# Attention value products in two passes instead of three, and a rewritten mixer order, in an fp32-accurate encoder layer

## The reference, cut to what matters

```python
h = _rms(x, g_mix[l]); z = h @ w_in[l]          # q | k | v | f | gate a | gate b
y_a = _window_attention(q, k, v, sink[l], rel_bias) @ w_branch_a[l]
y_b = _fourier_mix(f) @ w_branch_b[l]
x = x + (gate_a * y_a + gate_b * y_b) @ w_out[l]
```

## Time and profile before

| | us |
|---|---|
| median of three runs | 1013.02 |
| the profiled execution, whole | 1014.11 |
| its span from first to last instruction | 1012.3 |
| PE busy in the span | 997.7 (99%) |
| PEld busy | 885.7 (87%) |
| DVE busy | 679.0 (67%) |
| ACT busy | 440.1 (43%) |
| granted PE clock, mean | 0.995 of 2.4 GHz |

### The profile page before, as it was taken

The page is one execution under the profiler, slowest core; times in us unless marked ns, Lnnn a source line. Parts: engine busy times, 40 slices in busy tenths (PEclk is TensorE's granted clock), DMA queues, the critical chain, the costliest instruction groups (busy, mean ns, idle before and its releaser), DMA issues. The chain is left out here.

```text
span 1012.3 us, 16276 instructions
## 1 busy us (share of the span) xinstructions
PE 997.7 (99%) x5872; PEld 885.7 (87%) x5872; DVE 679.0 (67%) x924; ACT 440.1 (43%) x656; POOL 198.1 (20%) x113
## 2 busy tenths in 40 slices
PE   8999999999999999999999999999999999999997
PEld 7789999999788888888888888888999999978887
DVE  5778999999534346667765555458899999943332
ACT  5344444446322325346664334334445454633322
POOL 2452333340011110000000001324234333001101
PEclk9999999999999999999999999999999999999999
DMA  6423334323433364212213343322333332333222
GB/s 210 132 66 94 116 92 120 87 83 96 124 96 90 115 171 125 63 42 62 63 42 89 98 124 104 104 84 72 96 108 100 110 97 83 89 117 96 88 68 84
DMA packets 191816, 98.81 MB, mean 98 GB/s; under 512 B 13384, under 2 KB 190616, under 8 KB 191648
## 3 DMA queue, kind: packets, MB, share of 16 engines
q1 hardware_dynamic: 190560, 95.50, 32.3%
q10 hardware_dynamic: 1216, 2.78, 0.8%
HBM read 96.15 MB, written 2.11 MB: 97 GB/s over the span
## 5 line engine op out<-in xcount | busy, mean ns | idle before, releaser
L575 ACT ACTIVATE w_hi<-raw 128x1024 fp32r<-128x1024 f32 (+2 forms) x202 | 181.5, 902 | 231.6 <-PE bank L1496 155.2
L953 DVE TENSOR_TENSOR w_lo<-raw,w_hi 128x1024 fp32r<-128x1024 f32 (+2 forms) x138 | 150.0, 1089 | 145.7 <-ACT w_hi L575 144.2
L1595 PE MATMUL bank<-t_lo,w_hi 128*128 128x256 f32 x896 | 224.7, 283 | 0.0
L1593 PE MATMUL bank<-t_hi,w_hi 128*128 128x256 f32 x896 | 224.6, 283 | 0.0
L1595 PEld LDWEIGHTS bank<-t_lo,w_hi 128*128 128x128 f32 x896 | 172.0, 192 | 0.2
L1593 PEld LDWEIGHTS bank<-t_hi,w_hi 128*128 128x128 f32 x896 | 172.0, 192 | 0.2
L1430 POOL TENSOR_TENSOR ssum<-ssum,sq 128x512 f32<-128x512 f32 x27 | 41.4, 1533 | 535.2 <-ACT sq L612 534.4
L1599 PE MATMUL bank<-t_hi,w_lo 128*128 128x256 f32 x896 | 144.0, 283 | 0.0
L1484 PE MATMUL bank<-a_hi,w_hi 128*128 128x512 f32 (+1 forms) x374 | 140.6, 380 | 1.7 <-ACT a_hi L575 1.7
L1485 PE MATMUL bank<-a_lo,w_hi 128*128 128x512 f32 (+1 forms) x374 | 139.4, 377 | 0.0
L1599 PEld LDWEIGHTS bank<-t_hi,w_lo 128*128 128x128 f32 x896 | 123.6, 192 | 0.0
(11 more groups left out here) (230 smaller groups left out, 1494.6 us busy)
## 6 DMA issues: line engine op xcount, KB each, us to landing
raw<-in_w_down_dram SPq DMA_DIRECT2D x48, 384.0 KB, 3.0
raw_b<-in_w_up_dram SPq DMA_DIRECT2D x64, 256.0 KB, 3.7
raw<-in_w_up_dram SPq DMA_DIRECT2D x64, 256.0 KB, 3.6
raw<-in_w_up_dram SPq DMA_DIRECT2D x24, 512.0 KB, 3.9
raw<-in_w_in_dram SPq DMA_DIRECT2D x22, 512.0 KB, 3.7
raw<-in_w_down_dram SPq DMA_DIRECT2D x32, 128.0 KB, 2.2
raw<-in_w_out_dram SPq DMA_DIRECT2D x8, 512.0 KB, 3.4
x_rows<-in_x_dram SPq DMA_DIRECT2D x4, 512.0 KB, 7.8
```

The lines of the kernel that those rows point to most:

```text
L575: return nc.scalar.activation(dst, src, ACT.Copy, scale=scale)
L953: vec.tensor_tensor(w_lo[:, s, 0:nk, :], raw[:, s, 0:nk, :], w_hi[:, s, 0:nk, :].bitcast(F32), ALU.subtract).then_inc(w_lo_ready, 1)
L1593: nc.tensor.matmul(out_ap, w_hi[:, slot, at_ + k, :], hi[:, k, :], start=first and k == 0, stop=False, skip_group_check=not first)
L1595: nc.tensor.matmul(out_ap, w_hi[:, slot, at_ + k, :], lo_[:, k, :], start=False, stop=False, skip_group_check=not first)
```

## The change

v is kept in one tile `v_st` with a stationary block for each group: for group 0 columns 0 to 63 are v_hi and 64 to 127 are v_lo, for group 1 the other way round. `values` then takes two products, v_st x pt_hi and v_st x pt_lo, and leaves the part of v_hi in one half of the partitions of bank 3 and the part of v_lo in the other. (The lo x lo part comes with it.) The halves are added by two new operations at the last `values` of a unit: ACT copies the v_lo half of the bank to the other half of the partitions of `y_t` (`o_shifted`), DVE adds the bank's v_hi half to it (`o_added`). A new step `keep u`, one or more steps later in the list, has ACT copy the sum to `qo_hi` and DVE write `qo_lo`. The next unit's first `values` waits for `o_added` instead of `o_lo_ready`. The split of v is two operations on each engine instead of one. The list is rewritten, `B_B` starts with bank 0, and three waits follow it.

```diff
-B_B = [1, 0, 7]
+B_B = [0, 1, 7]
 MIXER:
-    positions 2; channels 3; q 2; turn_v; positions 3; q 3;
-    scores 0 0; scores 0 1; gate_b 0 0 0; gate_b 0 0 1; scores 0 2; scores 0 3; max 0; gate_b 0 0 2; exp 0;
+    positions 2; channels 3; q 2; turn_v; positions 3; scores 0 0; scores 0 1; q 3;
+    gate_b 0 0 0; scores 0 2; scores 0 3; max 0; gate_b 0 0 1; gate_b 0 0 2; exp 0;
     scores 1 0; normalize 0; gate_b 0 0 3; gate_b 0 1 0; scores 1 1; turn 0 0; turn 0 1; scores 1 2;
-    gate_b 0 1 1; values 0 0; scores 1 3; max 1; values 0 1; exp 1; normalize 1; gate_b 0 1 2; gate_b 0 1 3;
-    branch_b 0 0 0; sigmoid 0;
-    scores 2 0; scores 2 1; turn 1 0; branch_b 0 0 1; turn 1 1; branch_b 0 1 0; values 1 0; values 1 1;
-    scores 2 2; scores 2 3; max 2; take_b 0 0; exp 2; normalize 2; branch_b 0 1 1; gate_b 1 0 0; gate_b 1 0 1;
+    gate_b 0 1 1; values 0 0; scores 1 3; max 1; gate_b 0 1 2; values 0 1; exp 1; normalize 1; gate_b 0 1 3;
+    keep 0; branch_b 0 0 0; sigmoid 0;
+    scores 2 0; scores 2 1; turn 1 0; branch_b 0 0 1; turn 1 1; branch_b 0 1 0; values 1 0; scores 2 2; scores 2 3;
+    values 1 1; max 2; take_b 0 0; exp 2; normalize 2; keep 1; branch_b 0 1 1; gate_b 1 0 0; gate_b 1 0 1;
     take_b 0 1; gate_b 1 0 2; gate_b 1 0 3; turn 2 0; turn 2 1;
-    scores 3 0; scores 3 1; gate_b 1 1 0; values 2 0; turn 2 2; values 2 1; scores 3 2; scores 3 3; max 3;
-    exp 3; normalize 3; gate_b 1 1 1; gate_b 1 1 2; gate_b 1 1 3; values 2 2; sigmoid 1;
+    scores 3 0; scores 3 1; gate_b 1 1 0; values 2 0; turn 2 2; scores 3 2; scores 3 3; values 2 1; max 3;
+    exp 3; normalize 3; gate_b 1 1 1; gate_b 1 1 2; values 2 2; gate_b 1 1 3; keep 2; sigmoid 1;
     scores 4 0; branch_b 1 0 0; turn 3 0; turn 3 1; scores 4 1; branch_b 1 0 1; values 3 0; turn 3 2;
-    values 3 1; scores 4 2; scores 4 3; max 4; exp 4; take_b 1 0; branch_b 1 1 0; normalize 4; values 3 2;
-    branch_b 1 1 1; gate_b 2 0 0;
-    scores 5 0; scores 5 1; take_b 1 1; gate_b 2 0 1; turn 4 0; turn 4 1; gate_b 2 0 2; gate_b 2 0 3;
-    values 4 0; values 4 1; turn 4 2; scores 5 2; scores 5 3; max 5; exp 5; normalize 5; gate_b 2 1 0;
-    values 4 2; gate_b 2 1 1; gate_b 2 1 2; gate_b 2 1 3; branch_b 2 0 0; turn 5 0; turn 5 1;
-    scores 6 0; scores 6 1; values 5 0; turn 5 2; values 5 1; scores 6 2; scores 6 3; max 6; exp 6;
-    branch_b 2 0 1; values 5 2; normalize 6; branch_b 2 1 0; branch_b 2 1 1; sigmoid 2; take_b 2 0; take_b 2 1;
+    scores 4 2; scores 4 3; values 3 1; max 4; exp 4; take_b 1 0; branch_b 1 1 0; normalize 4; values 3 2;
+    branch_b 1 1 1; keep 3; gate_b 2 0 0;
+    scores 5 0; scores 5 1; take_b 1 1; gate_b 2 0 1; turn 4 0; turn 4 1; gate_b 2 0 2; values 4 0; gate_b 2 0 3;
+    turn 4 2; values 4 1; scores 5 2; scores 5 3; max 5; exp 5; normalize 5; gate_b 2 1 0;
+    values 4 2; gate_b 2 1 1; keep 4; gate_b 2 1 2; gate_b 2 1 3; branch_b 2 0 0; turn 5 0; turn 5 1;
+    scores 6 0; scores 6 1; branch_b 2 0 1; values 5 0; turn 5 2; scores 6 2; scores 6 3; values 5 1; max 6; exp 6;
+    branch_b 2 1 0; values 5 2; normalize 6; branch_b 2 1 1; keep 5; sigmoid 2; take_b 2 0; take_b 2 1;
     gate_b 3 0 0; gate_b 3 0 1; turn 6 0;
     scores 7 0; turn 6 1; gate_b 3 0 2; scores 7 1; values 6 0; scores 7 2; scores 7 3; values 6 1; max 7;
-    exp 7; normalize 7; gate_b 3 0 3; gate_b 3 1 0; ...
+    exp 7; normalize 7; gate_b 3 0 3; keep 6; gate_b 3 1 0; ...
-    ... values 7 1; branch_b 3 1 1; sigmoid 3; take_b 3 0; take_b 3 1;
+    ... values 7 1; branch_b 3 1 1; keep 7; sigmoid 3; take_b 3 0; take_b 3 1;

 ACT, last values of a unit:
-    copy(qo_hi[rows_v, :, block nb], banks[B_O][rows_v, :]).then_inc(o_hi_ready, 1)
+    if u == 0: act.wait_ge(y_lo_ready, N_FGROUPS)
+    if u >= N_KV: act.wait_ge(o_lo_ready, u - N_KV + 1)
+    copy(y_t[half_rows(kv), :], banks[B_O][half_rows(1 - kv), :]).then_inc(o_shifted, 1)
+ACT, keep u:
+    act.wait_ge(o_added, u + 1)
+    copy(qo_hi[half_rows(kv), :, block nb], y_t[half_rows(kv), :]).then_inc(o_hi_ready, 1)
 DVE, last values of a unit:
-    dve.wait_ge(o_hi_ready, u + 1); lo(qo_lo[...], banks[B_O][rows_v, :], qo_hi[...]).then_inc(o_lo_ready, 1)
+    dve.wait_ge(o_shifted, u + 1)
+    vec.tensor_tensor(y_t[half_rows(kv), :], banks[B_O][half_rows(kv), :], y_t[half_rows(kv), :], ALU.add).then_inc(o_added, 1)
+DVE, keep u:
+    dve.wait_ge(o_hi_ready, u + 1)
+    lo(qo_lo[...], y_t[half_rows(kv), :], qo_hi[...]).then_inc(o_lo_ready, 1)
 PE, values:
-    if b == 0 and u >= 1: pe.wait_ge(o_lo_ready, u)
+    if b == 0 and u >= 1: pe.wait_ge(o_added, u)
     pe.wait_ge(pt_hi_ready, t + 1)
-    nc.tensor.matmul(o_bank, v_hi[:, blk, :], pt_hi[:, t % 2, :], ...)
-    nc.tensor.matmul(o_bank, v_lo[:, blk, :], pt_hi[:, t % 2, :], ...)
+    nc.tensor.matmul(o_bank, v_st[:, kv, blk, :], pt_hi[:, t % 2, :], ...)
     pe.wait_ge(pt_lo_ready, t + 1)
-    nc.tensor.matmul(o_bank, v_hi[:, blk, :], pt_lo[:, t % 2, :], ...).then_inc(pt_used, 1)
+    nc.tensor.matmul(o_bank, v_st[:, kv, blk, :], pt_lo[:, t % 2, :], ...).then_inc(pt_used, 1)
 PE, gate_b, first quarter of granule n:
-    pe.wait_ge(out_read, O_B + n - 2 if n else O_B)
+    pe.wait_ge(out_read, O_B + n - 2 if n > 1 else O_B - 1 + n)
 PE, loop behind the mixer list:
-    pe.wait_ge(out_read, o - 3 + SLOTS * pair)
+    pe.wait_ge(out_read, o - (2 if j == 2 else 3) + SLOTS * pair)
```

More of the change, by code:

```diff
@@ L185 @@
-    turn 7 1; branch_b 3 0 0; branch_b 3 0 1; values 7 0; branch_b 3 1 0; values 7 1; branch_b 3 1 1;
+    exp 7; normalize 7; gate_b 3 0 3; keep 6; gate_b 3 1 0; gate_b 3 1 1; gate_b 3 1 2; gate_b 3 1 3; turn 7 0;
+    turn 7 1; branch_b 3 0 0; branch_b 3 0 1; values 7 0; branch_b 3 1 0; values 7 1; branch_b 3 1 1; keep 7;
     sigmoid 3; take_b 3 0; take_b 3 1;
@@ L325, in build @@
         kp_lo, _ = reuse("kp_lo", [P, N_KV, SEQ], F32R)
-        v_hi, _ = reuse("v_hi", [P, TB, P], F32R)
-        v_lo, _ = reuse("v_lo", [P, TB, P], F32R)
+        v_st, _ = reuse("v_st", [P, N_KV, TB, P], F32R)
         bias, bias_at = reuse("bias", [P, N_HEADS, 3 * BLK], F32)
@@ L372, in build @@
         proj_hi_ready, tab_hi_ready, exp_ready = sem("proj_hi_ready"), sem("tab_hi_ready"), sem("exp_ready")
+        o_shifted, o_added = sem("o_shifted"), sem("o_added")
         pt_hi_ready, o_hi_ready, ab_hi_ready = sem("pt_hi_ready"), sem("o_hi_ready"), sem("ab_hi_ready")
@@ L851, in _ @@
                         act.wait_ge(v_turned, 1)
-                        copy(v_hi[:, :, :], banks[B_CH][:, :]).then_inc(v_hi_ready, 1)
+                        v_rows = banks[B_CH][:, :].rearrange("p (t d) -> p t d", t=TB)
+                        for v in range(N_KV):
+                            last = copy(v_st[:, v, :, half_rows(v)], v_rows[:, :, half_rows(v)])
+                        last.then_inc(v_hi_ready, 1)
                     elif kind == "channels":
@@ L884, in _ @@
                         if b == len(window(nb)[0]) - 1:
-                            rows_v = slice(kv * HD, (kv + 1) * HD)
                             act.wait_ge(pt_used, turn_index(u, b) + 1)
-                            copy(qo_hi[rows_v, :, nb * BLK:(nb + 1) * BLK],
-                                 banks[B_O][rows_v, :].rearrange("p (c q) -> p c q", c=GQ)
-                                 ).then_inc(o_hi_ready, 1)
+                            if u == 0:
+                                act.wait_ge(y_lo_ready, N_FGROUPS)
+                            if u >= N_KV:
+                                act.wait_ge(o_lo_ready, u - N_KV + 1)
+                            copy(y_t[half_rows(kv), :], banks[B_O][half_rows(1 - kv), :]).then_inc(o_shifted, 1)
+                    elif kind == "keep":
+                        u = step[1]
+                        nb, kv = u // N_KV, u % N_KV
+                        act.wait_ge(o_added, u + 1)
+                        copy(qo_hi[half_rows(kv), :, nb * BLK:(nb + 1) * BLK],
+                             y_t[half_rows(kv), :].rearrange("p (c q) -> p c q", c=GQ)).then_inc(o_hi_ready, 1)
                     elif kind == "gate_b" and step[3] == 3:
@@ L1278, in _ @@
                         dve.wait_ge(v_hi_ready, 1)
-                        lo(v_lo[:, :, :], banks[B_CH][:, :].rearrange("p (t d) -> p t d", t=TB),
-                           v_hi[:, :, :]).then_inc(v_lo_ready, 1)
+                        v_rows = banks[B_CH][:, :].rearrange("p (t d) -> p t d", t=TB)
+                        for v in range(N_KV):
+                            last = lo(v_st[:, v, :, half_rows(1 - v)], v_rows[:, :, half_rows(v)],
+                                      v_st[:, v, :, half_rows(v)])
+                        last.then_inc(v_lo_ready, 1)
                     elif kind == "channels":
@@ L1343, in _ @@
                         if b == len(window(nb)[0]) - 1:
-                            rows_v, cols = slice(kv * HD, (kv + 1) * HD), slice(nb * BLK, (nb + 1) * BLK)
-                            dve.wait_ge(o_hi_ready, u + 1)
-                            lo(qo_lo[rows_v, :, cols],
```

(21 more changed lines are left out.)

1 line of the change is left out of this document (removed).

## The result

The changed kernel is slower. Its median is 1020.46 us over six runs (1018.73 to 1022.84), against 1013.2 for the kernel before over six runs in the same measurement. The ratio is 1.0078, with a 95% interval of 1.0065 to 1.0090. So the change costs 7.3 us by the medians and 7.9 (6.6 to 9.1) by the ratio. A second measurement of the same kernel gave 1.0081 (1.0068 to 1.0095).

What follows compares the result with a forecast made beforehand. PE was taken to set the time, busy 158.5 of 160 us in the mixer. Net waits of 10.35 us less 4.5 for twenty removed products gave +5.8, a median of 1018.8 us, range 1011.8 to 1022.3.

Steps and rivals of the forecast that it cites:

- Items 1 and 2: Start: scores 0 0 wait 1.1 for v_lo, scores 0 3 wait 2.0 for q 3's rest; net +1.6 us.
- Item 3: Unit 1: chain of 6.3 against PE's 5.2 until turn 1 0, +1.0; later pt_lo 0.25 more.
- Item 4: Unit 2: values 2 0 wait about 0.65 for pt_lo (0.3 before), scores 3 2 wait 0.4; +0.75 us.
- Item 5: Values 3 0, keep 2 before sigmoid 1: wait 1.2, and 0.45 for pt_lo; +1.55 us.
- Item 6: Values 4 0 with one gate step above it instead of two: DVE 4.35 against PE 3.0, +1.35 us.
- Item 7: Unit 4's last block: gate_b 2 0 3 moved later, 3.7 against PE's 3.2, and exp 5 later too; +0.65 us.
- Item 8: Values 5 0, keep 4 before gate_b 2 1 3 on ACT: wait 1.7, 0.35 behind it for scores; net +1.3 us.
- Item 9: Units 5 and 6: 0.8 up to turn 6 0; keep 5 delays pt_lo and scores 7 1's reading by 1.1; +1.9 us.
- Rival (a): Later holes do not open, PE gains 4.5 and pays only 1.6 at the start: 1010.1 us, faster; chance 0.14.
- Rival (b): About half of the later holes open: 1013 us, no change; chance 0.10.
- Rival (d): The removed products' time is not saved: 4.5 more, 1023 us; chance 0.14 together with the clock rival.
- Rival (c): Clock falls once or twice behind the waits, 1.2 to 1.7 each: 1020.0 to 1022.2; 0.14 with the products-not-saved rival.

Runs made afterwards that it cites:

- s1: Kernel before with three products and the old list, only the start and the banks new: ratio 1.0024, stretch 111.4 without its clock fall.
- p1: Kernel before without the product v_lo x pt_hi and nothing in its place, old list: ratio 0.9979, mixer stretch 107.9 us.
- n2: Kernel before with the new list, banks and waits, without v_lo x pt_hi and nothing in its place: ratio 1.0038, stretch 112.0 without its clock fall.
- e1: Changed kernel with the old list, banks and waits, keeps placed late: ratio 0.9984 to the kernel before, mixer stretch 108.4 us.
- e3: Changed kernel with only the keeps moved later, behind max u+2: ratio 1.0044 to the kernel before, stretch 112.5 without its clock fall.
- e2: Kernel before, three products, with the new list (without keep), new banks and waits: ratio 1.0069, stretch 113.8 without its clock fall.
- e4: Changed kernel with only the start put back (q 3 first again): ratio 1.0055 to the kernel before, stretch 113.6 without its clock fall.
- c3: Two products, late keeps, old list with covering gate and branch steps moved earlier from the start, new banks: ratio 1.0028 to the kernel before, stretch 114.1.
- c2: Two products, late keeps, old list and banks, covering steps moved earlier only from values 3 0 on: ratio 0.9989 to the kernel before, stretch 108.7.
- b1: Two products, late keeps, old list, with sigmoids later and exp 5 behind values 4 2: ratio 0.9987 to the kernel before, stretch 108.85.
- b2: Two products, late keeps, old list, with exp 5 behind values 4 2 and values 1 1 one step later: ratio 0.9978, 1010.6 us.

## Why the prediction was right, and where it was short

The sign and the mechanism were right: the median came out at 1020.46 against 1018.8 forecast, inside the range, and every hole listed under "What would show it" is there.

- **Items 1 and 2**: waits of 1.10 and 1.91, forecast 1.1 and 2.0. Net of what stood there (1.27) it is +2.07, forecast +1.6; alone in the kernel before they cost 1.8 (s1).
- **Item 3**: 1.09 at turn 1 0, forecast 1.0. The 0.25 for later `pt_lo` did not show: values 1 1 has no stall over 0.15 in the kernel after.
- **Item 4**: 0.94 and 0.30, less 0.30 before, is 0.94; forecast 0.75.
- **Item 5**: 1.53 for `pt_hi` and 0.41 for `pt_lo`, 1.94; forecast 1.55. The wait of `keep 2` for the addition (0.49) was missing from the chain.
- **Item 6**: 1.59, forecast 1.35. **Item 7**: 0.62, forecast 0.65 with turn 5 0, of which nothing over 0.15 showed.
- **Item 8**: 1.68, less 0.72, is 0.96; forecast 1.3. The main term was right (1.52 against 1.7), the 0.35 behind it is 0.17.
- **Item 9**: 0.77 + 0.22 + 0.60 = 1.6, forecast 1.9.
- **Unit 7, SP's loads, the tail, each costed at nothing**: confirmed. No stall of over 0.15 stands behind scores 7 3, and the tail takes 471.27 us in both.
- **The term that was missing**: items 1 to 9 measured +10.8 net (13.1 less 2.3) against 10.35, but the stalls under 0.15 grew by 0.8 as well ("rest"). The product right behind a wait is itself late: in the kernel after, the one that follows the product at scores 0 3 starts 0.10 late, and at values 2 0 it is 0.11. I had priced that for one restart, not for fourteen stalls. With it, 10.8 + 0.8 - 4.5 = +7.0 (before rounding) for 5.8.
- **The step that was wrong without hurting the sum** is the reading behind "What is removed". I took 0.227 us per product as won and put the loss of its cover into single items. p1 and n2 show that the cover is most of it: of 4.5 us, 1.7 to 1.8 are left. The trace before had it in plain sight, since `pt_lo` already arrived last at one place, behind two products that it had as cover. The forecast of the change came out because the items counted those waits; my forecast of p1, 3.2 us, was too good by 1.5. There is some luck in the sum too: items 1, 2, 4, 5 and 6 were 1.3 us short, and items 3, 8 and 9 0.8 too long.
- **On the Trainium skill's 131 ns per product** (TensorE: Matmul & The Clock Gate, Back-to-back issue gap): no run shows it. Products of 512 columns start 0.227 us apart in every profile at full clock. That 20 of them are worth only 1.8 us by the grid is another matter: p1's trace shows waits in their place, and not a faster stream.
- **Rival (a)**, later holes don't open, fell: items 3 to 9 cost 8.7 us net, forecast 8.75. **Rival (b)** fell with it. **Rival (d)**, the products' time is not saved, fell as it was priced: 4.5 more than the forecast is 1023, and the stretch is explained to 0.1 us with the products' time counted as saved. **Rival (c)**, the clock falls too, is open for this kernel: neither of its two profiles has a fall in the mixer, and four other kernels have one at the same wait.

## What to carry to other kernels

In a stream kept full by hand, count what a removed instruction covers before you count its time: look at the last wait behind it, and the gain is what is left of the slot once that wait has taken its share. An operation added to a chain should go as late in its engine's order as its reader allows; here the same ACT copy and DVE subtraction cost at most 0.5 us late (e1 against p1) and 4.1 us more early (after against e3). A step moved as cover for one engine carries its part on every other engine with it, so read all queues at the new place.

## What the runs showed of the hardware that I had not expected

**The clock can fall around a single wait.** Sums over stretches with columns as in the earlier trace rows, in s1, around the wait at scores 0 3:

```profile
441.50:444.50 3.00, 1.09 (x7) 0.77 (x6) 2.31 (x5) 2.66 (x4) 0.00 (x0) 1.00 0.27 80
444.50:447.90 3.40, 3.40 (x9) 2.74 (x10) 1.13 (x7) 1.80 (x7) 0.00 (x0) 0.50 0.03 9
447.90:451.00 3.10, 3.10 (x16) 2.56 (x15) 1.42 (x7) 0.41 (x4) 0.00 (x0) 1.00 0.00 0
```

PE was busy for 1.1 of 3 us, then dense again, and the granted clock is 0.50 (the 1.2 GHz level) for the 3.4 us that follow. Products start 0.43 us apart there instead of 0.227, some eight of them, which is the 1.6 us taken off above. The same fall stands in the profiles of e2, e3 and n2 at the same place, in e4 1.6 us behind the wait at values 5 0, and for 6.8 us in c3, from 0.9 us before the end of its wait of 3.07:

```profile
450.90:457.70 6.80, 5.86 (x20) 5.09 (x21) 2.95 (x10) 1.20 (x2) 0.00 (x0) 0.50 0.05 15
```

The kernel after has the same wait, and neither of its two profiles shows the fall:

```profile
440.00:443.50 3.50, 1.59 (x9) 1.23 (x8) 2.81 (x5) 2.94 (x4) 0.00 (x0) 1.00 0.25 75
443.50:447.00 3.50, 3.50 (x19) 2.93 (x18) 1.23 (x8) 2.17 (x9) 0.00 (x0) 1.00 0.01 2
```

So the wait alone doesn't decide it. The unprofiled runs of the kernel after reach to 1022.84 with a mean granted clock of 0.991 (0.996 in the profiled one). I estimate from the two means that PE had 10 us more at the lower level there, some three more falls, but no trace of those runs exists to show where. Another of its runs took 1021.46 at 0.997, so not every long run is one with more falls. In before, e1, p1, c2, b1 and b2, whose longest stalls are 1.3 us or less, no mixer has a fall. The Trainium skill (TensorE: Matmul & The Clock Gate, HAM oscillation) says that idle stretches between bursts send the clock back. The traces agree in part: five falls stand behind single stalls of 1.5 to 2.1 us inside dense work and one over a wait of 3.07, but the same stalls passed without one in the kernel after, and the early fall of the earlier trace rows came behind small products with a single wait of 0.25 us. Six of the fourteen profiles here have that early fall and eight have not. What decides it for one execution stays open.

**A copy of 64 partitions costs what one of 128 costs**: from a bank ACT's mean is 589 ns for 64x512 and 593 for 128x512, and DVE's subtraction takes 687 and 684. `keep`'s copy of 64x512, which reads `y_t`, takes 0.63 us, and the addition of 64x512 from a bank 0.68.
